# Neighbourhood attention of a two-block layer kernel: bias table laid out by tile, gates transposed in place of outputs

## The reference

```
def _neighbourhood_attn(q, k, v, rpb):      # 16 rows x 64 columns of tokens
    ...
    rpb_col = rpb[:, :, col_idx]
    mask = jnp.asarray(col_valid[:, :, None, :])
    ...
        bias = rpb_col[:, row_idx].transpose(0, 2, 3, 1, 4)
        sc = jnp.where(mask, sc + bias.astype(jnp.float32), -jnp.inf)
        p = jax.nn.softmax(sc, axis=(-2, -1)).astype(v.dtype)
        o = jnp.einsum('bhjqkc,bkjchd->bjqhd', p, v_band)
...
        o_b = o_b * jax.nn.silu(g_b)
        mixed = jnp.concatenate([o_a, o_b], axis=-1)
        x = x + mixed @ w_out[l]
    return _rmsnorm(x, final_norm_gain)
```

## Time and profile before

| | us |
|---|---|
| median of three runs | 2136.7 (2135.45 to 2138.93) |
| the profiled execution | 2139.72 |
| its span | 2137.9 |
| PE busy in the span | 1918.5 (90%) |
| DVE, ACT, POOL busy | 1024.1, 838.0, 392.0 |

### The profile page before, as it was taken

One profiled execution on the slowest core, in us unless ns is written; L12 is line 12 of the kernel. 1 busy time (PEld: TensorE's weight loads), 2 busy tenths in 40 slices (PEclk: granted clock), 3 DMA queues, 4 the chain that ended last, 5 costly groups with the idle time before them and its releaser, 6 DMA issues.

```text
span 2137.9 us, 39696 instructions
## 1 busy us (share of the span) xinstructions
PE 1918.5 (90%) x16401; PEld 1620.7 (76%) x16401; DVE 1024.1 (48%) x2378; ACT 838.0 (39%) x1812; POOL 392.0 (18%) x393
## 2 busy tenths in 40 slices
PE   7964889998779679998999999999999989999997
PEld 6963778887668569997777777777777777888897
DVE  5751777714224152612555444454444456785503
ACT  5321777724334151422333333333333245444423
POOL 2540000020110002322212222122222010001211
PEclk9986999999889899999999999999999999999999
DMA  4110000042222222232222121122211220004431
GB/s 168 41 27 12 5 1 1 1 109 77 80 62 75 75 96 102 82 92 87 66 77 61 56 71 53 56 65 74 61 57 57 68 74 21 11 21 138 141 145 79
DMA packets 146716, 141.10 MB, mean 66 GB/s; under 512 B 21893, under 2 KB 132041, under 8 KB 146537
## 3 DMA queue, kind: packets, MB, share of 16 engines
q1 hardware_dynamic: 146456, 138.10, 20.9%
q0 software_dynamic: 80, 0.47, 0.1%
HBM read 101.83 MB, written 36.89 MB: 65 GB/s over the span
## 4 chain that ended last, share of the span: by engine, by line
PE 67%; DVE 7%; ACT 4%; issue 2%; POOL 2%; SPq 2%; DMA 1%; DVEq 0%; POOLq 0%; ACTq 0%
PE ps L974 8%; PE ps L681 7%; PE ps L976 6%; PE ps L975 6%; PE ps L682 6%; PE ps L683 6%; PE ps L1077 4%; PE ps L1261 3%; PE ps L1284 3%; PE ps L1114 3%; PE ps L1143 2%; PE ps L769 1%; PE ps L1271 1%; SPq L3058 1%; PE ps L1063 1%
## 5 line engine op out<-in xcount | busy, mean ns | idle before, releaser
L681 PE MATMUL ps<-t,t 128*128 128x256 f32 (+2 forms) x1392 | 440.3, 316 | 57.5 <-issue 50.3
L682 PE MATMUL ps<-t,t 128*128 128x256 f32 (+2 forms) x1392 | 432.0, 310 | 0.0
L683 PE MATMUL ps<-t,t 128*128 128x256 f32 (+2 forms) x1392 | 431.0, 310 | 0.0
L2733 POOL TENSOR_TENSOR t<-t,t 128x512 fp32r<-128x512 f32 x183 | 237.7, 1313 | 815.6 <-ACT t L1362 797.3
L681 PEld LDWEIGHTS ps<-t,t 128*128 128x128 f32 x1392 | 271.9, 195 | 77.5 <-issue 62.5
L974 PE MATMUL ps<-t,t 128*128 128x512 f32 (+2 forms) x720 | 298.3, 414 | 1.2 <-ACT t L1643 1.2
L683 PEld LDWEIGHTS ps<-t,t 128*128 128x128 f32 x1392 | 271.6, 195 | 11.9
L682 PEld LDWEIGHTS ps<-t,t 128*128 128x128 f32 x1392 | 272.1, 195 | 10.8 <-issue 0.2
L976 PE MATMUL ps<-t,t 128*128 128x512 f32 (+2 forms) x720 | 269.0, 374 | 0.0
L975 PE MATMUL ps<-t,t 128*128 128x512 f32 (+2 forms) x720 | 268.6, 373 | 0.0
L1362 ACT ACTIVATE t<-t 128x512 fp32r<-128x512 f32 x186 | 109.9, 621 | 151.1 <-DMA t<-in_w_in 84.3
(11 more groups left out here) (259 smaller groups left out, 3202.7 us busy)
## 6 DMA issues: line engine op xcount, KB each, us to landing
t<-in_w_in SPq DMA_DIRECT2D x53, 512.0 KB, 5.2
zgate_spill<-t SPq DMA_DIRECT2D x20, 512.0 KB, 3.2
t<-in_x SPq DMA_DIRECT2D x16, 512.0 KB, 9.6
t<-zgate_spill SPq DMA_DIRECT2D x16, 512.0 KB, 3.6
feat_spill<-t SPq DMA_DIRECT2D x13, 512.0 KB, 3.2
t<-in_w_in SPq DMA_DIRECT2D x6, 1024.0 KB, 5.3
t<-band_bias SPq DMA_DIRECT2D x128, 48.0 KB, 2.3
t<-values_and_gates SPq DMA_DIRECT2D x96, 64.0 KB
```

The lines of the kernel that those rows point to most:

```text
L681: e.matmul(dst, lh, rh, start=k == 0, stop=False)
L682: e.matmul(dst, lh, rl, start=False, stop=False)
L683: m = e.matmul(dst, ll, rh, start=False, stop=k == n - 1)
L2733: e.tensor_tensor(WLO[wslot(b)][:, o], WST[:, o], WHI[wslot(b)][:, o].bitcast(F), ALU.subtract).then_inc(w_lo.sem, w_lo.up((b, p)))
```

## The change

- The table. A tile UNSEEN of mask values is set once in SBUF. Six transfers from it fill `band_d` and sixteen fill a new table `bias_d` (`tile_bias`), which holds for each head and half the 128 query rows by 1152 biases as a tile needs them. After the 40 bias transfers, 48 transfers from `band_d` to `bias_d` lay the biases out. All but the 40 are paced: each waits for the one before the last.
- `load_biases` becomes one transfer. POOL's memsets of BIAS go.
- Gates in place of outputs. `band_gates` multiplies the gates of a tile with the reciprocals (tokens on partitions), PE transposes the result into the other half of the bank of the values, ACT copies it (GTT), and `band_output` is one product of the values' bank with it, into MIXT with channels on partitions. Nothing of B is then transposed at the end; `band_part` splits MIXT by halves of the tokens, for pairs 0 to 2 within the tiles of pair 3 (the low half on POOL).
- The QK products use banks 0, 1, 7 and 2, and a tile's scores wait for their own half of the queries alone. DVE takes the left-over outputs ahead of the splitting of QK. VBAND has a counter for each of its four bands, and GBP is loaded ahead of it.
- The first two tiles of the output projection are put among the last tiles of attention B.

```diff
-        MIXB = sb([128, 8, 512], F, W0 + 16 * KB)
+        MIXT = sb([128, 4, T], F, W0 + 16 * KB)
...
+        MIXED = [(p, r) for p in range(3) for r in range(2)]
...
             def band_scores(m):
...
-                for what, half in QK:
+                for what, half in QK[0:2] + (("q", t // 4),):
...
             def band_value(m):
                 t = m % 8
-                ob = bank_at(("ot", m), 6, (value_t, m))
-                w.wait_ge(*d_vb[m // 8 - 8])
+                ob = bank_at(("ot", m), 6, (attn_v, (m, "out")))
+                w.wait_ge(*attn_v[m, "gates"])
+                e.transpose(ob[:, 128:256], GSC[m % 2][:, :], ident)
+                w.wait_ge(*d_vb[t % 4][m // 8 - 8])
...
+            def output_product(n, i, ps, hi, lo):
+                w.wait_ge(*tile_hi["b", 3, i // 4])
+                w.wait_ge(*tile_lo["b", 3, i // 4])
+                w.wait_ge(*band_lo[2, 1])
+                by_tokens(ps, i, hi, lo, 8, ("wo1", n, i))
...
                 for x, (what, half) in enumerate(QK):
-                    ps = bank_at(("band", what, p, half), (7, 0, 1, 7)[x], (qk_hi, (what, p, half)), (qk_lo, (what, p, half)))
+                    ps = bank_at(("band", what, p, half), (0, 1, 7, 2)[x], (qk_hi, (what, p, half)), (qk_lo, (what, p, half)))
...
-            for x in range(3):
-                band_output(B_Z + 29 + x)
+            hi, lo = enter()
+            for x in range(2):
+                ps = bank_at(("wo1", 0, x), x, (resid_v, (0, x)))
+                output_product(0, x, ps[:, 0:256], hi, lo)
                 if x == 0:
                     band_turn(B_Z + 31)
-                if x < 2:
-                    band_value(B_Z + 30 + x)
-                    for t in (2 * x, 2 * x + 1):
-                        turn_mixed(t, 1, 2 * x + t % 2)
+                band_value(B_Z + 30 + x)
             PE.end("attention b")
...
+            def band_part(p, r):
+
+                w.wait_ge(*attn_v[B_Z + 8 * p + 4 * r + 3, "out"])
+                w.wait_ge(*dense_mm["q", 3, 1])
+                e.activation(by_band(AH[:, 4 + p, half512(r)]), banded(MIXT[:, p, half512(r)]), ACT.Copy).then_inc(tile_hi.sem, tile_hi.up(("b", p, r)))
...
-                for s in range(2):
-                    hs = slice(64 * s, 64 * s + 64)
-                    e.scalar_tensor_tensor(out=MIXB[:, t, 128 * p + 64 * s:128 * p + 64 * s + 64], in0=psum(("o", m))[:, hs], scalar=RIN[:, c + s:c + s + 1],
-                                           in1=GBP[:, t, hs], op0=ALU.mult, op1=ALU.mult).then_inc(attn_v.sem, attn_v.up((m, s, "out")))
...
+                e.tensor_tensor(GSC[m % 2].rearrange("p (s c) -> p s c", s=2), GBP[:, m % 8, :].rearrange("p (s c) -> p s c", s=2),
+                                bc(RIN[:, c:c + 2], 2, 64), ALU.mult).then_inc(attn_v.sem, attn_v.up((m, "gates")))
+
+            def band_output(m):
+                ob = psum(("ot", m))
+                w.wait_ge(*value_t[m])
+                e.tensor_tensor(MIXT[:, m // 8 - 8, tile128(m % 8)], ob[:, 0:128], GTT[m % 2][:, :], ALU.mult).then_inc(attn_v.sem, attn_v.up((m, "out")))
...
-            e.dma_start(band_d.rearrange("h q k d c -> (h q k d) c"), bass.AP(a["consts"].tensor, C_CAUS + 64, [[0, 8 * 16 * 3 * 15], [1, 32]])).then_inc(
-                d_band.sem, d_band.up("masked"))
+            def band_table(n, dst, src):
+
+                if n > 1:
+                    w.wait_ge(*d_band[n % 2][n - 2])
+                e.dma_start(dst, src).then_inc(d_band[n % 2].sem, d_band[n % 2].up(n))
+
+            w.wait_ge(*zero_p["unseen"])
+            for n in range(6):
+                band_table(n, band_d.rearrange("h q k d c -> (h q k) (d c)")[tile128(n // 2), 240 * (n % 2):240 * (n % 2) + 240], UNSEEN[:, 0:240])
+            for n in range(16):
+                band_table(6 + n, bias_d[n // 2, n % 2].rearrange("q (k x) -> q k x", k=3), bc(UNSEEN[:, :], 1, 3))
...
+            for r in range(2):
+                for q in range(8):
+                    o, d = (32 * min(q, 4), 7 - max(q, 4)) if r else (32 * max(q - 4, 0), 7 - min(q, 4))
+                    for k in range(3):
+                        band_table(22 + 24 * r + 3 * q + k, bass.AP(bias_d.tensor, 128 * 1152 * r + 16 * 1152 * q + 384 * k + o, [[2 * 128 * 1152, 8], [1152, 16], [1, 256]]),
+                                   bass.AP(band_d.tensor, 480 * k + 32 * d, [[16 * 1440, 8], [1440, 16], [1, 256]]))
...
-                for s in range(2):
-                    for q in range(8):
...
+                e.dma_start(BIAS[r].rearrange("q s k x -> q s (k x)"), bias_d[2 * p:2 * p + 2, r].rearrange("s q x -> q s x")).then_inc(
+                    d_bias[r].sem, d_bias[r].up(p))
...
-            w.wait_ge(*d_band["all"])
+            for n in (68, 69):
+                w.wait_ge(*d_band[n % 2][n])
```

More of the change, by code:

```diff
@@ L1601, in act_program @@
             for n in range(2):
-                wt.enter()
-                for i in range(NT):
+                if n:
+                    wt.enter()
+                for i in range(0 if n else 2, NT):
                     wt.tick(12)
@@ L3107, in sp_program @@
                     load_biases(p + 1, 1)
+            wt.enter()
+            for _ in range(2):
+                wt.tick(12)
             for q in EVERY:
```

179 lines of the change are left out of this document (87 added, 92 removed).

## The result

The changed kernel takes 2024.45 us (median of 4 runs, 2022.4 to 2027.08) against 2137.81 us (4 runs, 2135.45 to 2139.48): ratio 0.9471, 95% interval 0.9454 to 0.9489. The profiled execution took 2022.47 us (span 2020.7).

A forecast was written before the change was run, and what follows sets the result against it. PE was taken to bound the kernel, so gains come from its waits. 47.8 + 64.5 + 2.0 + 2.5 = 116.8 us off the profiled 2139.72 gives 2022.9, or 2020 us for a median; range 2010 to 2038.

The forecast's parts named there:

- The pause: Gate projections: PE's 47.77 us without instructions, blamed on SP's long transfer of 5760 pieces; replacing it gains 47.8 us.
- no idle of PE above 3 us between 140 and 160: Gate projections and start of attention A: sign that PE's long wait for instructions is gone.
- Rival (b): Gate projections: PE's stop for instructions stays, having another cause than the long transfer; 2068 us, chance 0.10 including a partial case.
- Rival (c): Bias table: its 48 copies are too slow, the table is late for attention B and the kernel slower; 2529 us, chance 0.03.
- rival (d): Attention B: PE never waits for tile 7 or bank 0, and 2.7 us more count in attention A; 2014 us, chance 0.11.
- The changes of pair: Attention B, between pairs: earlier weights and new order cut each change to 25.3 us; gain 64.5 us in all.
- the landing of the weights: Change of pair: weights land 4.75 us after issue, plus 3.2 us for the biases ahead of them.
- Rival (a): Changes of pair: biases hold up the weights, PE waits 3 to 5 us each and runs slower after; about 2032 us, chance 0.16.
- Inside the tiles: Pair 3 of attention B: DVE's cheaper output saves 0.4 us for each of five tiles; gain 2.0 us.
- The end of attention B: From T, end of DVE's last split of A, into the output projection: 7.0 us against 9.5; gain 2.5 us.
- the wait for bank 0: Output projection, fourth product: PE waits 3.2 us until the first product has been added to the residual.
- Shift as a whole: Norms, recurrence and the rest behind attention B: they only move earlier, with no gain of their own.

The follow-up runs named there:

- before_paced: Kernel before, with only the long transfer of 5760 pieces replaced by six 120 KB transfers from SBUF, at most two in flight; 2094.32 us against 2140.07.
- before_own_source: Kernel before, long transfer kept as 5760 pieces in one go, but each read from SBUF instead of one place in device memory; 2093.54 us, ratio 0.9775.
- before_parts: Kernel before, long transfer cut into eight of 720 pieces from the same place in device memory, at most two in flight; 2090.43 us, ratio 0.9768.
- after_weights_first: Changed kernel, with the second load of biases of a pair issued behind the next weights instead of ahead; 2020.81 us, ratio 0.9451.
- after_all_queries: Changed kernel, with scores of tiles 0 to 3 waiting for both halves of the queries again; 2030.87 us, ratio 0.95.
- after_turn_first: Changed kernel, with the last tile's turn and tile 30's values ahead of the output projection's first product; 2018.97 us, ratio 0.944.

## Why the prediction was right, and where only by chance

**The pause.** Right, and shown by before_paced: the whole gain comes with the transfer. It took both properties of the transfer: with fast pieces (before_own_source) or with few queued at once, in shorter transfers (before_parts), the pause is gone. Two readings of the rows were wrong without harm to the forecast. Instructions did not come again as the transfer ended, near 200, but at 188.6, and of the three blocks of rows 5 the first moved at 199.9, ahead of the forty small transfers. The forecast took 47.8, and the first maximum did come 47.3 sooner; it missed that PE, early now, idles 3.17 us for ACT's first exponential and then runs at half clock, which makes the third scores 1.4 us late. That idle time also breaks a check that the prediction named ("no idle of PE above 3 us between 140 and 160"), though with ACT as its releaser and not "issue". Rival (b) has fallen. Rival (c) as well: 48 copies took 74.52 us (77 forecast, 1.55 each, far from 4.0), and the table was ready some 124 us early (113 forecast). So has rival (d): PE waited 1.71 and 0.97 us for tile 7 and 2.94 for bank 0.

**The changes of pair.** The mechanism was right; the term of 65.0 (64.5 and the 0.5 of DVE's split) became 61.5. The step that was mis-sized is the landing of the weights: 4.75 us after issue was taken from the kernel before, but behind after_weights_first's issue (477.71) it is 6.1, so 1.3 more, with gates and biases issued behind them (that these cost the 1.3 is not shown). With 3.5 for the biases, ACT goes on 11.1 us after the issue of the last store (475.94 to 487.05; the prediction's 7 to 10 count from there, the 11.8 of after_weights_first from ACT's last gate at 475.27). PE's wait was "0 to 1 us", with 0.5 taken; it is 1.71, 0.97 and 0. Rival (a) named this price and what follows it, half the clock for a while, and the first change paid it: 28.36 = 24.83 + 1.71 + 1.8. So (a) came true in one of three places and in small, and the 1.8 is chance in part: the same wait cost 0.3 beyond its length in after_all_queries.

**Inside the tiles.** Pair 3's tiles follow each other in 4.25 us against 4.70; 0.4 had been worked out, and the stretch gives the 1.5 that were left for it.

**The end of attention B.** Wrong: -0.3 instead of +2.5. The start (T + 1.14) and the wait for bank 0 (2.94; 3.2 forecast) were sized well. What failed is the 2.9 us taken for the first product: behind 3.33 us of idle time it took 5.25, and the values, the last split and the loads of the residual stand behind it, so that the fourth product came at T + 18.45 and not T + 15.4. after_turn_first shows it: with that idle time filled, the product takes 2.97. The miss is not one execution's: in the six profiles with this part of the changed kernel the row of the table has 61.3 to 62.7 us after the change. The sum has a slip of its own: by its terms PE is at the fourth product at T + 12.5 and the addition done at T + 15.1, so the wait is 2.6 and the gain 3.1, not 3.2 and 2.5.

**The rest.** "Shift as a whole" was wrong by 8.4 us, to the good, and that alone brings the sum back to the forecast. This tail has the same instructions in every kernel. In twelve profiles it took 1287.0 to 1296.9 us: 1292.3 to 1296.9 in the four with the old attention B, 1287.0 to 1292.3 in the eight with the new. Between the two profiles 6.6 of the 8.4 us arise in the last quarter, from 1541 us of the changed kernel on, where the kernel before falls to the lower clock at three places at which the changed one keeps the full clock (near 1740, 1938 and 2037 us; the changed one falls at one, near 1611, where the other does not). The first of them, behind a wait of 2.57 us in the kernel before and of 1.79 in the changed one:

```profile
1740.00:1743.00 3.00, 2.87 (x9) 2.90 (x10) 0.00 (x0) 0.49 (x1) 0.03 (x1) 0.50 0.59 183
```

```profile
1630.00:1633.00 3.00, 3.00 (x19) 3.00 (x19) 0.87 (x4) 1.37 (x3) 0.00 (x0) 1.00 0.93 262
```

So part of the 8.4 is the two executions compared. Whether some 4 us of it belong to the change (the means of the two sorts of profiles differ by 4.4) stays open: no run changed anything that would tell it.

## What to carry to other kernels

A transfer of many small pieces that all read one place in device memory can be slow (82 us for 720 KB here), and if it is put in at once it can starve an engine of instructions that has nothing to do with it; read it off from "issue" idle time beside a stretch without instruction packets, and cut it into paced parts or give each partition its own source. Put weights that an engine waits for ahead of data that is needed later, in the queue as well as in SP's order. When you add up waits, price a wait of PE not by its length alone but with the matmuls at half clock that may follow it (0.2 to 2.35 us here), and fill it with real work that is due soon anyway. Before you compare two single profiles, see how much a stretch with the same instructions differs from run to run.

## What was not expected of the hardware

- 720 KB in 5760 pieces of 128 bytes moved at 9 to 11 GB/s from one place of device memory, with the DMA engines about 5% busy, and at 173 GB/s from SBUF.
- The same slow pieces, two transfers of 720 in flight, cost PE at most 0.90 us at a time, against 47.77 in one transfer. A block of instructions came 15 to 21 us later with two such transfers in flight, and 62 us later with the long one.
- PE's clock: in the changed kernel it was granted at 0.66 over the 5 us that follow a wait of 1.71 us, and the change of pair took 1.8 us more than the wait explains; with a wait of 0.97 in the second change the excess was 0.2. In after_all_queries the full clock followed a wait of 1.72 at the place of the 1.71, and the excess was 0.3.
